# Twenty modulation pairs leave the DeltaNet levels for the hybrid projection units

## The reference, cut to what matters

```python
mod = jnp.split(s_lat @ mod_w[layer] + mod_b[layer], 6, axis=-1)   # s_lat = silu(c), one vector
h = modulate(rms_norm(x, norm_mix_pre[layer]), mod[0], mod[1])
# layer 0: hybrid mixer: one projection of h (and of the context), then two mixers on it
p = h @ w_in
o_lat, o_ctx = bidir_deltanet(lat_in, ctx_in)      # chunked gated delta rule, two directions
b_lat = blocked_attention(q_lat, k_all, v_all)     # softmax attention
y = jnp.concatenate([a_lat, b_lat], axis=-1) @ w_out
x = x + mod[2] * rms_norm(y, norm_mix_post[layer])
# then the gated MLP (mod[3] to mod[5]); layer 1: short convolution mixer and MLP, its own mod
```

## Time and profile before

| | us |
|---|---|
| time, median of 3 runs (1820.99 to 1821.25) | 1821.21 |
| the profiled execution's own time | 1819.29 |
| its span in the profile | 1817.4 |
| hybrid projection units | 60 to 226.8 of the span |
| DeltaNet, from `dn_ready` | 245.1 to about 633 |
| attention | to about 800 |

### The profile page before, as it was taken

The page is one execution under the profiler, slowest core; times in us unless marked ns, Lnnn a source line. Parts: engine busy times, 40 slices in busy tenths (PEclk is TensorE's granted clock), DMA queues, the critical chain, the costliest instruction groups (busy, mean ns, idle before and its releaser), DMA issues.

```text
span 1817.4 us, 22614 instructions
## 1 busy us (share of the span) xinstructions
PE 1718.3 (95%) x9080; PEld 1429.1 (79%) x9080; DVE 982.6 (54%) x1242; ACT 704.5 (39%) x1058; POOL 323.4 (18%) x227
## 2 busy tenths in 40 slices
PE   8899997989988998989999999999999999999998
PEld 2788897889988955567788888887888688888886
DVE  2643277867697567757544444446446744444222
ACT  2432433344444478733433333223223244433321
POOL 3000014553464346512000000110002100000000
PEclk9899998999999968999999999999999999999999
DMA  8213041212221324032222332321322122332221
GB/s 337 68 54 81 16 151 47 71 47 70 93 70 48 117 70 139 24 93 83 80 93 93 105 100 84 104 94 52 108 96 93 47 93 92 104 103 87 87 87 64
DMA packets 153918, 161.14 MB, mean 89 GB/s; under 512 B 11383, under 2 KB 151144, under 8 KB 152680
## 3 DMA queue, kind: packets, MB, share of 16 engines
q1 hardware_dynamic: 153344, 159.74, 27.2%
q10 hardware_dynamic: 488, 0.18, 0.0%
HBM read 157.81 MB, written 2.10 MB: 88 GB/s over the span
## 4 chain that ended last, share of the span: by engine, by line
PE 82%; DVE 8%; ACT 4%; issue 2%; POOL 2%; DMA 0%; DVEq 0%; SPq 0%; ACTq 0%; POOLq 0%
PE ps L461 18%; PE ps L463 18%; PE ps L462 18%; PE ps L719 3%; PE ps L698 3%; PE ps L724 3%; ACT mod_raw_c L1107 2%; PE ps L509 1%; PE ps L810 1%; PE ps L827 1%; PE ps L829 1%; PE ps L828 1%; PE ps L784 1%; DVE w_lo L1389 1%; DVE dn_bl L1605 1%
## 5 line engine op out<-in xcount | busy, mean ns | idle before, releaser
L1389 DVE TENSOR_TENSOR w_lo<-w_raw,w_hi 128x2048 fp32r<-128x2048 f32 x100 | 229.1, 2292 | 512.7 <-ACT w_hi L1053 512.7
L461 PE MATMUL ps<-h_hi,w_hi 128*128 128x512 f32 x968 | 377.2, 390 | 0.4 <-DVE w_lo L1389 0.4
L462 PE MATMUL ps<-h_lo,w_hi 128*128 128x512 f32 x968 | 376.7, 389 | 0.0
L463 PE MATMUL ps<-h_hi,w_lo 128*128 128x512 f32 x968 | 376.7, 389 | 0.0
L1053 ACT ACTIVATE w_hi<-w_raw 128x2048 fp32r<-128x2048 f32 x100 | 191.2, 1913 | 320.9 <-PE ps L463 306.0
L1911 POOL TENSOR_TENSOR mod_raw_c<-mod_raw_c 128x1024 f32<-128x1024 f32 (+2 forms) x120 | 189.0, 1578 | 141.9 <-ACT mod_raw_c L1107 134.9
L461 PEld LDWEIGHTS ps<-h_hi,w_hi 128*128 128x128 f32 x968 | 181.7, 188 | 38.3 <-DVE w_lo L1389 0.8
L462 PEld LDWEIGHTS ps<-h_lo,w_hi 128*128 128x128 f32 x968 | 181.7, 188 | 37.6
L463 PEld LDWEIGHTS ps<-h_hi,w_lo 128*128 128x128 f32 x968 | 181.7, 188 | 37.7
L461 PE MATMUL ps<-mid_hi,w_hi 128*128 128x512 f32 x338 | 132.9, 393 | 0.0
L463 PE MATMUL ps<-mid_hi,w_lo 128*128 128x512 f32 x338 | 131.8, 390 | 0.0
(11 more groups left out here) (331 smaller groups left out, 2789.1 us busy)
## 6 DMA issues: line engine op xcount, KB each, us to landing
w_raw<-in_ffn_w_up SPq DMA_DIRECT2D x44, 1024.0 KB, 5.1
mod_raw_c<-in_mod_w SPq DMA_DIRECT2D x40, 1024.0 KB, 5.3
w_raw<-in_ffn_w_down SPq DMA_DIRECT2D x16, 896.0 KB, 4.6
w_raw<-in_sc_w_in SPq DMA_DIRECT2D x12, 1024.0 KB, 5.2
w_raw<-in_hyb_w_in SPq DMA_DIRECT2D x9, 1024.0 KB, 5.4
mod_raw_a<-in_mod_w SPq DMA_DIRECT2D x8, 1024.0 KB, 16.2
w_raw<-in_ffn_w_down SPq DMA_DIRECT2D x8, 1024.0 KB, 5.0
w_raw<-in_sc_w_out SPq DMA_DIRECT2D x4, 1024.0 KB, 5.0
```

What stands on the lines that cost most here:

```text
L461: mm(dst, hi, xh[:, k0 + k, :], start=first and k == 0, stop=False)
L462: mm(dst, hi, xl[:, k0 + k, :], start=False, stop=False)
L463: i = mm(dst, lo, xh[:, k0 + k, :], start=False, stop=last and k == nk - 1)
L1389: V.tensor_tensor(wlo[s][:, :], raw[s][:, :], f32(whi[s][:, :]), ALU.subtract).then_inc(sem("w_lo"), 1)
```

## The change

Pairs 0 to 19 are handled during the hybrid projection, two for each of units 2 to 11. Each parity has one 8 KB buffer per partition (`mod_raw_e0` over the temporaries, `mod_raw_e1` over the context input). Even pairs are multiplied by ACT in eight instructions, odd pairs by DVE in one. POOL adds them, the last add into a ring of four sums, and PE makes their columns two units later. In the DeltaNet levels one pair is left in each of the first four chunk steps (products at level 1, all adds at level 3, columns at level 5). Pairs 24 to 39 keep their places. DVE waits for all forty early columns before `dn_ready`.

```diff
+        EARLY, LEVEL_PAIRS = 20, 4
+        def early_at(u):
+            return [j for j in range(EARLY) if j // 2 + 2 == u]
         def mod_at(q, lag):
-            return [j for j, q0 in enumerate(MOD_LEVEL) if q0 + lag == q]
+            return [j for j in range(EARLY, EARLY + LEVEL_PAIRS) if LEVELS * (j - EARLY) + 1 + lag == q]
 # SP
+            def load_early(j):
+                if j == 0:
+                    sp.wait_ge(sem("h"), 2 * KC)
+                elif j >= 2:
+                    sp.wait_ge(sem("mod_acc"), acc_c(j - 2))
+                sp.dma_start(mraw_e[j % 2][:, :, :], mod_source(j)).then_inc(sem(f"mod_e{j % 2}"), 16)
 ...
             for u in range(2, 12):          # after the weight load of unit u
+                for j in early_at(u - 2):
+                    load_early(j)
             sp.wait_ge(sem("tile"), 2 * U_WOUT)
 ...
+            for u in range(U_WOUT - 2, U_WOUT + 2):
+                for j in early_at(u):
+                    load_early(j)
-            for j in range(PAIRS):
+            for j in range(EARLY, PAIRS):
                 load_mod_pair(j)
 # PE, in step u after unit u's matmuls, ahead of the norm statistics
+            def mod_columns(pairs):
+                for j in pairs:
+                    pe.wait_ge(sem("mod_acc"), acc_c(j))
 ...
+                mod_columns(early_at(u - 2))
                 for e in ITEMS_IN.get(u - 1, ()):
                     item_stat(e)
 # ACT, at the end of step u (behind the squares)
+            def early_products(u):
+                for j in early_at(u):
+                    if j % 2 == 0:
+                        act.wait_ge(sem("mod_e0"), 16 * (j // 2 + 1))
+                        products(mraw_e[0])
 # DVE, in step u behind the taps or copies, ahead of recip(0) in step 11
+            def early_products(u):
+                for j in early_at(u):
+                    if j % 2:
+                        dve.wait_ge(sem("mod_e1"), 16 * (j // 2 + 1))
+                        V.tensor_tensor(mraw_e[1][:, :, :], mraw_e[1][:, :, :], bc(cvec[:, :, 0], UW), ALU.mult).then_inc(sem("mod_prod1"), 1)
 ...
             recip(2)
+            dve.wait_ge(sem("mod_done"), 2 * EARLY)
 # POOL
+            for j in range(EARLY):
+                mod_parts(j)
             pool.wait_ge(sem("rope_in"), 32)
```

More of the change, by code:

```diff
@@ L117, in hybrid_trunk @@
                   for i in range(MSLOTS)]
+        mraw_e = [view(place(f"mod_raw_e{i}", KC * UW, F32, a0), "p (k n) -> p k n", n=UW)
+                  for i, a0 in enumerate((tmp_at, R + 73 * K))]
+        macc = view(region("mod_sums", 4 * UW, 81), "p (j n) -> p j n", n=UW)
         hc_hi = view(region("hc_hi", KC * CTX, 57, F32R), "p (c t) -> p c t", t=CTX)
@@ L195, in landed @@
         def landed(j):
-            return 16 * (j // MSLOTS + 1)
+            return 16 * ((j - EARLY) // MSLOTS + 1)
+        def early_at(u):
+            return [j for j in range(EARLY) if j // 2 + 2 == u]
         def z_count(s, l, d):
@@ L205, in u_count @@
             return (s * (LEVELS - 1) + l) * 2 + d + 1
-        MOD_LEVEL = [LEVELS * (j // 4) + 2 * (j % 4) for j in range(DN_PAIRS)]
         def mod_block(i, lag):
-            return [j for j in range(DN_PAIRS, PAIRS) if 7 * (j - DN_PAIRS) // 4 + lag == i]
+            j0 = EARLY + LEVEL_PAIRS
+            return [j for j in range(j0, PAIRS) if 7 * (j - j0) // 4 + lag == i]
         def mod_at(q, lag):
-            return [j for j, q0 in enumerate(MOD_LEVEL) if q0 + lag == q]
+            return [j for j in range(EARLY, EARLY + LEVEL_PAIRS) if LEVELS * (j - EARLY) + 1 + lag == q]
         MOD_IN = ["mod_a0", "mod_a1", "mod_a2", "mod_a2", "mod_a3", "mod_a3", "mod_a4", "mod_a4"]
@@ L346, in _, with mod_source @@
             sp.dma_start(vrow[V_CCTX:V_CCTX + KC, 0, :], A["c_ctx"].rearrange("(c p) -> c p", p=P)).then_inc(sem("c_in"), 16)
+            def mod_source(j):
+                layer, part = divmod(8 + j, MODS // 2)
+                return A["mod_w"][layer].rearrange("(k p) n -> p k n", p=P)[:, :, part * UW:(part + 1) * UW]
+            def load_early(j):
[4 more added lines that the diff above has]
+                sp.dma_start(mraw_e[j % 2][:, :, :], mod_source(j)).then_inc(sem(f"mod_e{j % 2}"), 16)
             def load_mod_pair(j):
[L350 to L353, removed]
+                s = (j - EARLY) % MSLOTS
+                if j >= EARLY + MSLOTS:
                     sp.wait_ge(sem("mod_done"), 2 * (j - MSLOTS + 1))
-                sp.dma_start(mraw_c[s][:, :, :], src).then_inc(sem(f"mod_in{s}"), 16)
+                sp.dma_start(mraw_c[s][:, :, :], mod_source(j)).then_inc(sem(f"mod_in{s}"), 16)
             def raw_free(u):
@@ L481, in mod_column @@
                 mm(bank(7, 1, 16 + m), acc, ones[:, 0:1], start=True, stop=True).then_inc(sem("mod_done"), 1)
+            def mod_columns(pairs):
+                for j in pairs:
+                    pe.wait_ge(sem("mod_acc"), acc_c(j))
+                    acc = macc[:, j % 4, :] if j < EARLY else mraw_c[(j - EARLY) % MSLOTS][:, 0, :]
+                    for part in range(2):
+                        mod_column(16 + 2 * j + part, acc[:, part * P:(part + 1) * P])
             def sum_columns(sq, idx, n, first, last):
@@ L638, in _ @@
                 item_rows(e)
[L639 to L643, removed]
+            for u in range(U_WOUT - 2, U_WOUT + 2):
+                mod_columns(early_at(u))
             def gate_rows(s):
@@ L756, in _ @@
                     i.then_inc(sem("Sp"), 1)
-            for q in range(LEVELS * NT, LEVELS * NT + 5):
-                mod_columns(mod_at(q, 4))
             pe.wait_ge(sem("S"), 2 * NT)
@@ L1165, in _ @@
                     square(e)
+                early_products(u)
             group_sd(1)
@@ L1170, in _ @@
             group_sd(2)
+            for u in range(U_WOUT, U_WOUT + 2):
+                early_products(u)
             act.wait_ge(sem("gcv"), 3)
@@ L1200, in _ @@
                     for j in mod_at(s * LEVELS + l, 0):
-                        act.wait_ge(sem(f"mod_in{j % MSLOTS}"), landed(j))
-                        products(mraw_c[j % MSLOTS])
+                        act.wait_ge(sem(f"mod_in{(j - EARLY) % MSLOTS}"), landed(j))
+                        products(mraw_c[(j - EARLY) % MSLOTS])
                 for d in range(2):
@@ L1911, in mod_add, with mod_parts @@
                 G.tensor_tensor(dst, a, b, ALU.add).then_inc(sem("mod_acc"), 1)
-            def mod_half(n, slot):
-                w = 4 >> (n % 3)
-                mod_add(n, slot[:, 0:w, :], slot[:, 0:w, :], slot[:, w:2 * w, :])
+            def mod_parts(j):
+                early = j < EARLY
+                slot = mraw_e[j % 2] if early else mraw_c[(j - EARLY) % MSLOTS]
+                pool.wait_ge(sem("mod_prod1" if early and j % 2 else "mod_prod"), j // 2 + 1 if early else j - EARLY // 2 + 1)
+                mod_add(3 * j, slot[:, 0:4, :], slot[:, 0:4, :], slot[:, 4:8, :])
+                mod_add(3 * j + 1, slot[:, 0:2, :], slot[:, 0:2, :], slot[:, 2:4, :])
+                if early and j >= 4:
+                    pool.wait_ge(sem("mod_done"), 2 * (j - 3))
+                mod_add(3 * j + 2, macc[:, j % 4, :] if early else slot[:, 0, :], slot[:, 0, :], slot[:, 1, :])
             post_squares(0)
@@ L1959, in _ @@
                         G.tensor_tensor(rope_tile(l - 1), rope_tile(l - 1), cosT[:, :], ALU.mult).then_inc(sem("rcos"), 1)
[L1960 to L1964, removed]
+                    for j in mod_at(s * LEVELS + l, 2):
+                        mod_parts(j)
+            for j in range(EARLY + LEVEL_PAIRS, PAIRS):
+                mod_parts(j)
             for j in range(4):
```

9 lines of the change are left out of this document (removed).

## The result

The changed kernel takes 1859.49 us (median; 1859.44 to 1862.8) beside 1821.23 for the kernel before: ratio 1.021, 95% interval 1.0193 to 1.0229. It is slower by 38 us, where 15 was forecast; the time lies outside the range of 1816 to 1850. The profiled spans are 1857.8 and 1817.4, 40.4 apart.

The account below looks back on a forecast made before the run. PE was taken to bound the kernel, with 82% of the chain. Projection loss 24 plus gap loss 30 minus DeltaNet gain 39 gave +15 us, a forecast of 1836 us, range 1816 to 1850.

Parts of the forecast that it names:

- the projection's loss: Projection units up to 11: weights queued behind early loads on SP make unit 11 end 24 us later.
- DeltaNet's gain: DeltaNet chunk steps: 20 of 24 pairs leave, saving PE's waits, stretched masks, columns and slow clock; 39 us.
- the gap's loss: Unit 11's end to `dn_ready`: late loads, products and adds of pairs 16 to 19 delay the reciprocal; 30 us.
- rival C: PE idles in the projection and the gap, each restart at 1.2 GHz costing about 2 us: +8, 1844 us; chance 0.15.
- The aside on the six loads: Gap: the six loads that stood there, 6.8 MB or 18 us at 312 GB/s, are issued behind, early enough for pair 20.
- the loop of the weights behind SP's waits: Projection: next weights wait in SP's queue for POOL's pair sums; some 32 us for two steps against PE's 12.6 each.
- The meetings on the port: Projection: POOL's adds and DVE's splits or products wait for each other, 2.3 us a step; without them loss 18, not 24.
- A: Projection: weights come in time, PE loses only the columns, 4 us; total -5, 1816 us; chance 0.12.
- B: Projection and gap: no POOL and DVE meeting on the port, losses 18 and 28; total +7, 1828 us; chance 0.18.
- D: DeltaNet gives only its waits and columns, 18 to 25 us; total +31, 1852 us; chance 0.10 together with E.
- E: Early pairs summed so late that DeltaNet step 0 still waits; near 1855 us; chance 0.10 together with D.

Follow-up runs that it names:

- b1: Kernel before with all three adds of pairs 0 to 19 made 8 columns wide, everything else left in the DeltaNet levels: 1798.28 us, ratio 0.9862.
- g16: Changed kernel with pairs 16 to 19 put back into the DeltaNet levels (16 early pairs, eight level pairs five levels apart): 1850.27 us.
- e2: Changed kernel with SP issuing the weights of unit k+1 ahead of the early loads of unit k-2: 1854.73 us.
- c1: Changed kernel with weights first, loads of pairs 16 to 19 before the wait for unit 11, and DVE's products of steps 8 and 9 behind gate work: 1832.19 us.
- e4: Changed kernel with DVE's products of steps 8 and 9 (pairs 13 and 15) behind those steps' gate inputs and decay: 1844.3 us, ratio 1.0115.
- c3: c1 with the last loads behind the wait again and the first two adds of each early pair 8 columns wide instead of 256: 1821.7 us.
- c2: c1 with every early pair one unit earlier, units 1 to 10 instead of 2 to 11: 1817.7 us, ratio 0.9970 to the kernel before.
- e1: Changed kernel without loads, products and adds of pairs 0 to 19, their columns summed over a constant: 1790.91 us, ratio 0.9853 to the kernel before.
- v12: c2 with 12 early pairs in units 1 to 6 and twelve level pairs three levels apart: 1826.4 us, ratio 1.0014 to the kernel before.

## Why the prediction was wrong

The sign, the three stages and two of the three terms held. The term that failed is **the projection's loss**: 24 us in the sum, 44.3 measured. The sizes:

| | forecast | measured |
|---|---|---|
| DeltaNet's gain | 39 | 36.0 |
| the gap's loss | 30 | 33.1 |
| the projection's loss | 24 | 44.3 |

*DeltaNet.* Right in place and near in size: 24.2 of 36.0 by the adds alone (b1); chunk steps 0 and 1 at 59.5 and 55.5 us, full clock. Step 2 with 60.2 is above the 57.5 worked out. One reading was off: POOL's 27 to 30 us a step are not nearly all pair work. Step 1 went from 27.4 to 12.7 with three pairs fewer, so four pairs are some 20 us of it. No term hangs on that.

*The gap.* The mechanism is seen in the trace: 29.3 of the 33.1 us stand ahead of the reciprocal, where 30 was forecast. g16 undoes 26.3 of them. The other 3.8 us of the changed kernel are slower norm rows behind the reciprocal: twelve took 2.90 us at 301.41. The same twelve before:
```profile
228.34 1.58 PE L618 MATMUL ps<-const,item_dev 128*128 128x128 f32 x12
```
In g16, whose gap ran slow as a whole, this is 6.8 us. I had given the clock to rival C. (The aside on the six loads is off too: 18 us at 312 GB/s are 5.7 MB, not 6.8. Nothing hangs on it.)

*The projection.* Here the mechanism was wrong, not only the size. I made the loop of the weights behind SP's waits the pace-maker. It is in the trace, and up to 212 us on time. SP's issues for units 7 and 8, and ACT's splits of units 7, 9 and 10, which don't follow PE:
```profile
154.06 0.58 SPq L399 DMA_DIRECT2D w_raw<-in_hyb_w_in  x1
169.07 0.58 SPq L401 DMA_DIRECT2D w_raw<-in_hyb_w_in  x1
163.02 1.92 ACT L1077 ACTIVATE w_hi<-w_raw 128x2048 fp32r<-128x2048 f32 x1 [7.42 <-issue]
192.46 1.91 ACT L1077 ACTIVATE w_hi<-w_raw 128x2048 fp32r<-128x2048 f32 x1 [3.42 <-issue]
212.41 1.92 ACT L1077 ACTIVATE w_hi<-w_raw 128x2048 fp32r<-128x2048 f32 x1 [6.26 <-issue]
```
Worked out were 154.5 and 169 for the issues, 163 for the weights of unit 7, 209.8 for those of unit 10. (One piece of that sum is off by 1 us: 163.93 to 172.2 less a split of 1.9 is 6.4, not 7.3.) But without this link little changes: e2 gained 3 us, and c1 over e4 1 to 2. What the runs put in its place, each counted from the start of its own projection: DVE's order 15 us (e4), POOL's adds 20 us (c1 to c3), the columns 7 (c3), the weights 1 to 2. These make 44.
The step that failed is how the loop was closed. The prediction has 16 us a step only because SP's queue puts the weights behind the loads. A loop of nearly that length is there without the weights: load 5.3, product 3.3 and adds 6.5 in one buffer are 15.1 us, more than PE's 12.6, so putting the weights first leaves POOL's sums nearly as late as they were: the loads of pairs 8 and 9 start at 177.39 in c1 and at 177.32 in the changed kernel. I had the three numbers (5.4, 3.3, and 4.7 with 2.3 for a meeting) and never added them for one buffer. Second, I named what stands behind a waiting load on SP, but not what stands behind a waiting product on DVE, `abt` and the decay; these 15 us were put at nothing. Third, the clock was left out of the sum: some 12 us of the 44.3 are slower matmuls. The columns I took at 4 us cost 7.
The meetings on the port were right in kind: DVE's odd products took 2.29 to 4.18 us, its splits up to 3.08 (2.29 without POOL). The Trainium skill ("SBUF — State Buffer", Who interferes with whom) says that a VectorE instruction with two SBUF inputs and a GpSimd instruction that reads SBUF contend, and the trace agrees: in c1 POOL's first two adds of a pair took 3.68 us with no such instruction beside them (260.56) and 5.62 beside a product (254.12).

*The rivals.* A needed the weights in time and a loss under 9 us: e2 had the first and not the second, so A's deciding point was the wrong place. B is out, since the meetings took place. C was right that the clock costs time and too low in its price, 8 us: some 12 in the projection and 3.8 in the gap. It expected PE idle for 3 to 7 us in five or six places; there were two waits of 11.67 and 6.68 us and four of 0.8 to 2.5. D and E are out: DeltaNet gave nearly what was counted, and `dn_ready` waited 0.66 us for the early columns.

## What to carry to other kernels

When work is moved onto idle engines, sum the whole loop of one buffer (load, product, adds, release) and compare it with the period of the stage; that each engine has room is not enough. For each instruction that is put into an in-order queue and can wait for a DMA, list what stands behind it and who waits for that: a copy of 0.25 us behind such a product cost the kernel more than ten. And move only as much as the stage's pace holds. With the same order of the queues, 14 pairs in units 1 to 7 gave 14 us, and 20 pairs in units 1 to 10 (c2) 4 us, none of it ahead of attention; 20 pairs in units 2 to 11 without the better order cost 38.

## What the runs showed of the hardware

The granted clock fell where PE never stopped. In b1, whose projection is that of the kernel before, and in e1, PE was busy 14.00 of 14.00 us at 0.76; the kernel before had 1.00 in its late units. b1, then e1:
```profile
192.00:206.00 14.00, 14.00 (x52) 11.48 (x52) 4.05 (x6) 7.16 (x12) 0.00 (x0) 0.76 0.00 0
```
```profile
192.00:206.00 14.00, 14.00 (x65) 12.24 (x64) 4.05 (x6) 8.78 (x12) 0.00 (x0) 0.76 0.00 0
```
PE had been busy without a gap since 78 us in both. In b1 the slow matmuls (0.63 us each instead of 0.39) begin right behind 24 of the one-column matmuls that sum the squares:
```profile
190.10 3.12 PE L567 MATMUL ps<-const,sqt 128*128 128x1 f32 x24
193.08 0.77 PE L461 MATMUL ps<-h_hi,w_hi 128*128 128x512 f32 x1
```
In e1 they begin at 181.14 and at 197.12, again behind columns and such sums. The kernel before has the same 24 at 187.35 and stays at full clock, so this is where it fell and not yet why. c1 has it too: busy 16.00 of 16.00 us at 0.87 (above). So a low clock can't be put down to the waits by itself.

Attention, which no edit touches, ran at 0.97, 0.92 and 0.86 in different traces, with the same work. After, before, v12:
```profile
720.00:875.00 155.00, 137.91 (x624) 99.36 (x623) 112.06 (x167) 102.46 (x200) 72.47 (x48) 0.97 0.31 89
```
```profile
680.00:835.00 155.00, 136.83 (x589) 98.47 (x588) 108.89 (x162) 97.99 (x190) 69.57 (x46) 0.92 0.30 89
```
```profile
690.00:850.00 160.00, 144.18 (x582) 104.20 (x580) 103.91 (x150) 86.58 (x163) 62.76 (x42) 0.86 0.28 81
```
The stretch behind DeltaNet took 1176.5 us (e2) to 1199.9 (v12). What sets the clock there stays open. For this kernel an edit of under 10 us is read from marks in the trace and not from one total.
